# Hybrid decoder block on one core: another order for the last attention jobs and the first feed-forward units

## Chip, cores and metric

The kernel runs on one NeuronCore of a Trainium2 chip. The metric is the device time of one execution in microseconds (us), as the median of several runs; before the change it is 583.53 us (three runs, 583.22 to 583.65).

## What is computed

One layer, with x of 512 tokens by 1024 (float32), cut to what matters here:

```python
h = rms_norm(x, g_mix_norm)
z = h @ w_in                      # q, k, v of 8 heads, gate logits, gMLP channels
o_attn = g0 * o_cmp + g1 * o_sel + g2 * o_win       # compressed, selected, window attention
o_mix = gelu(zu) * spatial(rms_norm(gelu(zv)))
o = concat([rms_norm(o_attn, g_out[:512]), rms_norm(o_mix, g_out[512:])])
x = x + o @ w_out
h = rms_norm(x, g_ffn_norm)
x = x + square(relu(h @ w_ff1)) @ w_ff2              # w_ff1 1024 x 4096, w_ff2 4096 x 1024
```

## The kernel before

Tokens lie in four tiles of 128 (t = 0 to 3). The five engines run programs of their own, each in its written order, and wait on counting semaphores. Every float32 product is made of three matmuls (`three`, lines 427 to 429) over operands split into a high and a low part: ScalarE writes the high part, VectorE the rest. Weights come by DMA in units of 128 x 1024 into a ring of four `raw` slots; `unit_hi` (line 1039, ScalarE) and `unit_lo` (line 1563, VectorE) split them.

The **attention** goes in steps over heads and branches on TensorE. Between the steps stand jobs, named by kind, token tile and half:

- ("attno", t, h): twelve matmuls that project the attention rows of tile t on half h of the model width. VectorE's `add` (line 1555) puts the result on the residual `xs`, and counts `added`.
- ("attn", t, 0): four transposes (line 1779) of the attention rows of tile t into a PSUM bank. They wait for `o_evac`, which VectorE counts after the last additions (`combine`, line 1543) of the tile's sums.
- ("ffn", t, i): four transposes of half i of the rows of tile t for the feed-forward, which VectorE's `ffn_rows` (line 1222) makes from `xs` when both the addition of ("attno", t, i) and the norm weights are there.

A transposed bank is taken out by `ht_hi_evac` (line 785, ScalarE) and `ht_lo_evac` (line 1228, VectorE), which count `ht_half` and `ht_done`; of some ("ffn", t, 0), listed in `RAWS`, also by `raw_keep` (line 1044, ScalarE) as plain float32. `turn_back` (line 2085) are two transposes that bring finished attention sums into token order, after ScalarE's `ot_keep` (line 1073).

Behind the attention's loop stand the jobs of `TAIL`, in this order on TensorE: ("attno",2,1) and the last `turn_back`, ("attn",3,0), ("ffn",2,0), ("ffn",1,0), ("ffn",1,1), ("attno",3,0), ("attno",3,1), ("ffn",3,0), ("ffn",2,1); then feed-forward unit 0, ("ffn",3,1), unit 1, unit 2 and so on.

The **feed-forward** is a seven-product scheme over two token blocks (tiles 0 and 1, tiles 2 and 3) and two halves of the inner width. A unit is one `raw` slot of weights: 24 matmuls of 128 x 256 (`first_unit`) for the first matrix. Units 0 to 3 belong to product P2 (rows 0 to 255, second half of the width: ("ffn",0,1) and ("ffn",1,1)), units 4 to 7 to P1, units 8 and on use sums of rows (`form`, `form_high`, `form_low`) and weights that GpSimd's DMA adds up in the `raw` slot (line 680). A unit n waits for `w_lo` of its weights; the load of unit n+4 waits for the same split.

The order of VectorE behind the loop: `ffn_rows(2,0)`, `add(attno,2,1)`, `ht_lo_evac(attn,3,0)`, `ffn_rows(2,1)`, `ht_lo_evac(ffn,1,0)` and `(ffn,1,1)`, `add(attno,3,0)`, `ffn_rows(3,0)`, `ht_lo_evac(ffn,2,1)`, `late_difference(2)` (line 1604, a difference of two transposed halves), `add(attno,3,1)`, `ffn_rows(3,1)`, `unit_lo(2)`, `ht_lo_evac(ffn,3,1)`, `late_difference(3)`, `unit_lo(3)`. ScalarE: a wait for the last additions and the squares of attention tile 3 (line 770), `ht_hi_evac(attn,3,0)`, `raw_keep(2,0)`, for i = 0, 1 `raw_keep(1,i)` and `ht_hi_evac(ffn,1,i)`, squares of tile 2, `raw_keep(3,0)`, `ht_hi_evac(ffn,2,1)`, `unit_hi(2)`, `ht_hi_evac(ffn,3,1)`, `unit_hi(3)`, squares of tile 3. The weights of units 0 and 1 are split inside the attention's loop.

Of the kernel before, what the change touches and what calls it, by code (L numbers as in the profile page):

```python
# [14 lines left out]
NT = SEQ // P  # L15
# [36 lines left out]
NS = len(SPLITS)  # L52
# [27 lines left out]
N1 = BLOCK * sum(r[0] == 1 for r in ROUNDS)  # L80


def unit(n):

    stage, product, block, q, adding = ROUNDS[n // BLOCK]
    return stage, product, block * BLOCK + n % BLOCK, q, adding
# [17 lines left out]
def results_of(n):  # L104
# [13 lines left out]

RAWS = [(0, 0), (0, 1), (2, 0), (1, 0), (1, 1), (3, 0)]
FORMED = ["S1late2", "S1late3", "S3", "S2", "S4"]
FSPLIT = ["S1", "S2", "S4", "S3"]
FORM_STEPS = {5: "S3", 6: "S2", 7: "S4"}
# [9 lines left out]
KINDS = ["x", "mix", "attn", "ffn"]  # L134

HT = ([("x", u, k) for u in range(4) for k in range(2)] + [("mix", t, 0) for t in range(NT)]
      + [("attn", 0, 0), ("attn", 1, 0), ("ffn", 0, 0), ("ffn", 0, 1), ("attn", 2, 0), ("attn", 3, 0),
         ("ffn", 1, 0), ("ffn", 1, 1), ("ffn", 2, 1), ("ffn", 3, 1)])
HTN = {k: n for n, k in enumerate(HT)}


# [32 lines left out]
NV = len(STEPS)  # L174
# [37 lines left out]
def steps_of(k):  # L212
# [6 lines left out]
ENDS = {v + steps_of(k) - 1: k for k, v in JOBS.items()}  # L219
assert max(CHUNKS) < NV + LAG and len(CHUNKS) == sum(map(steps_of, JOBS))  # L220

TAIL = [("attno", 2, 1), ("attn", 3, 0), ("ffn", 2, 0), ("ffn", 1, 0), ("ffn", 1, 1), ("attno", 3, 0),
        ("attno", 3, 1), ("ffn", 3, 0), ("ffn", 2, 1), ("ffn", 3, 1)]
JOB_BANK = {k: JB[n % 2] for n, k in enumerate(JOBS)}
JOB_BANK.update({("ffn", 1, 0): 5, ("ffn", 1, 1): 6,
                 ("attno", 2, 1): 3, ("attn", 3, 0): 0, ("ffn", 2, 0): 4, ("ffn", 2, 1): 3, ("attno", 3, 0): 1,
                 ("attno", 3, 1): 2, ("ffn", 3, 0): 0, ("ffn", 3, 1): 1})
JOB = {k: n for n, k in enumerate(list(JOBS) + TAIL)}
JOB_KEY = list(JOB)
# [1 line left out]
ADD_NO = {k: n for n, k in enumerate(ADDS)}  # L231
# [4 lines left out]
def hybrid_block(nc, x, xt, w512, w_c, cmp_w1, cmp_w2, cmp_pe, sp_w, sp_b, g_cols, g_ffn, g_heads, g_sgu,  # L236
                 g_kc, rope, w_ff1, w_ff2, y):
    ctx = ExitStack()
    with ctx:
# [130 lines left out]
        w_hi, w_lo = sem("w_hi"), sem("w_lo")  # L370
# [37 lines left out]
        o_step, o_evac = sem("o_step"), sem("o_evac")  # L408
        job_done, added = sem("job_done"), sem("added")
        r2_step = sem("r2_step")  # L410
        raw_kept, formed = sem("raw_kept"), sem("formed")
# [49 lines left out]
        def job_taken(eng, k):  # L461
# [5 lines left out]
            else:  # L467
                eng.wait_ge(raw_kept, RAWS.index(k[1:]) + 1)

# [274 lines left out]
        def _(act):  # L744
# [34 lines left out]
            def ht_hi_evac(kind, t, i):  # L779
                if (kind, t, i) not in JOB:  # L780
                    act.wait_ge(filled, FILL["mixT", t, i] + 1)
                else:
                    act.wait_ge(job_done, JOB[kind, t, i] + 1)
                src, h, _ = halves_of(kind, t, i, ht_bank(kind, t, i))
                act.activation(h, src, ACT.Copy).then_inc(ht_half, 1)
# [255 lines left out]
            def raw_keep(t, i):  # L1041

                act.wait_ge(job_done, JOB["ffn", t, i] + 1)
                act.activation(ht_raw[:, 4 * i:4 * i + 4, t * P:t * P + P],
                               ps[:, JOB_BANK["ffn", t, i], :].rearrange("p (k s) -> p k s", k=4), ACT.Copy
                               ).then_inc(raw_kept, 1)
# [63 lines left out]
                    norm_sum("ffn", t, scr[:, :])  # L1110
            act.wait_ge(o_evac, 2 * NT)
            norm_sum("attn", 3, scr[:, 0:AW])
            ht_hi_evac("attn", 3, 0)
            raw_keep(2, 0)
            for i in range(2):
                raw_keep(1, i)
                ht_hi_evac("ffn", 1, i)
            act.wait_ge(added, ADD_NO["attno", 2, 1] + 1)
            norm_sum("ffn", 2, scr[:, :])

# [61 lines left out]
        def _(dve):  # L1182
# [34 lines left out]
            def ffn_rows(t, i):  # L1217

                cols = slice(i * AW, i * AW + AW)
                dve.wait_ge(grow_ffn_in, 16)  # L1220
                dve.wait_ge(added, ADD_NO["attno", t, i] + 1)
                dve.tensor_tensor(o_sb[:, t, cols], xs[:, t, cols], grow_ffn[:, cols], ALU.mult).then_inc(n_rows, 1)

            def ht_lo_evac(kind, t, i):
                n = HTN[kind, t, i]
                dve.wait_ge(ht_half, n + 1)
                src, h, l = halves_of(kind, t, i, ht_bank(kind, t, i))
                dve.tensor_tensor(l, src, h.bitcast(F32), ALU.subtract).then_inc(ht_done, 1)
# [317 lines left out]
            def add(kind, t, h):  # L1546

                c = slice(h * AW, h * AW + AW)
                dve.wait_ge(job_done, JOB[kind, t, h] + 1)
                if kind == "mixo":  # L1550
                    dve.wait_ge(x_again[t], 16)
                    dve.wait_ge(o_rstd, 1)
                else:
                    dve.wait_ge(o_rstd, t + 2)
                dve.scalar_tensor_tensor(out=xs[:, t, c], in0=ps[:, JOB_BANK[kind, t, h], :],
                                         scalar=stat(rstd, {"mixo": "mix", "attno": "attn"}[kind], t),
                                         in1=xs[:, t, c], op0=ALU.mult, op1=ALU.add).then_inc(added, 1)
# [8 lines left out]
            for w in range(NV + LEAD + LAG + BACK + 1):  # L1566
                s = w - LEAD
                k = ENDS.get(s)
# [22 lines left out]


            ffn_rows(2, 0)
            add("attno", 2, 1)
            ht_lo_evac("attn", 3, 0)
            ffn_rows(2, 1)
            ht_lo_evac("ffn", 1, 0)
            ht_lo_evac("ffn", 1, 1)

            def late_difference(t):  # L1600

                cut = (slice(None), slice(0, 4), slice(t * P, t * P + P))
                dve.wait_ge(raw_kept, RAWS.index((t, 0)) + 1)
                dve.tensor_tensor(ht_raw[:, 4:8, t * P:t * P + P], ht_raw[cut],
# [46 lines left out]
            def form(s):  # L1651

                dve.wait_ge(formed, FORMED.index(s))
                if s == "S3":
                    dve.wait_ge(raw_kept, len(RAWS))
                    dve.tensor_tensor(form_raw("S3"), form_raw("S2"), form_raw("S3"), ALU.subtract).then_inc(formed, 1)
# [102 lines left out]
        def _(pe):  # L1759
# [316 lines left out]
            def turn_back(i):  # L2076

                pe.wait_ge(ot_evac, i + 1)
                if i == 0:
                    wait_free(pe, LAST_FILL[3])  # L2080
                elif i % 2 == 0:
                    pe.wait_ge(o_evac, i // 2)
                for e in range(2):
                    c = i % 2 * 256 + e * P
                    mm = pe.transpose(ps[:, 7, c:c + P], ot_sb[:, i % 2, e, :], ident[:, :])
                mm.then_inc(back_done, 1)
# [15 lines left out]
            def job(k, c):  # L2102

                before = [p for p in JOB_KEY[:JOB[k]] if JOB_BANK[p] == JOB_BANK[k]]
                if c == 0 and before:
                    job_taken(pe, before[-1])
                if k in TRANSPOSED:
                    rows_t(k[0], k[1], (k[2],))
                else:
                    mm = project(*k, c)  # L2110
                    if c == 3:
                        mm.then_inc(job_done, 1)
# [18 lines left out]
                    turn_back((v - LAG - BACK) // 4)  # L2131

            pe.wait_ge(pt_lo, NV)
            for k in TAIL[:-1]:
                for c in range(4 if k in ADD_NO else 1):
                    job(k, c)
                if k == TAIL[0]:
                    turn_back(NV // 4 - 1)


            pe.wait_ge(o_evac, 2 * NT)

            def row_form(product):

                if product in ("P5", "P6", "P3"):
# [6 lines left out]
            def first_unit(n):  # L2152

                _, product, k, _, _ = unit(n)
                j = n % BLOCK
                h, l = row_form(product)
                for e in range(2):
                    for kt in range(4):
                        c = slice(512 * e + P * kt, 512 * e + P * kt + P)
                        mm = three(pe, psum_of(n)[:, e * TH:e * TH + TH], w_hi_sb[:, FS[j], c], w_lo_sb[:, FS[j], c],  # L2160
                                   h[:, kt, :], l[:, kt, :], kt == 0, kt == 3)
                mm.then_inc(w_used, 1)

            def wait_rows(product):

                if product == "P2":
                    pe.wait_ge(ht_done, HTN["ffn", 1, 1] + 1)
                elif product == "P4":
                    pe.wait_ge(ht_done, len(HT))
                elif product != "P1":  # L2170
                    pe.wait_ge(form_lo, FSPLIT.index({"P5": "S1", "P6": "S2", "P3": "S4", "P7": "S3"}[product]) + 1)
# [6 lines left out]
                else:  # L2178
                    pe.wait_ge(combined, COMBINED[BANK_FREE[product], k] + 1)

            for n in range(N1):
                r = n // BLOCK
                if r < 7 and n % BLOCK == 0:
                    wait_rows(unit(n)[1])
                if r >= 2:
                    bank_taken(n - 2 * BLOCK)
                elif n == 0:
                    pe.wait_ge(raw_kept, RAWS.index((2, 0)) + 1)
                elif n == BLOCK:
                    pe.wait_ge(raw_kept, len(RAWS))  # L2190
                    pe.wait_ge(formed, 2)
                    pe.wait_ge(added, len(ADDS))
                pe.wait_ge(w_lo, NS + n + 1)
                first_unit(n)
                if n == 0:
                    job(("ffn", NT - 1, 1), 0)

            def piece(n, e, i):

# [10 lines left out]
            for n in range(N1, NU - BLOCK):  # L2210
                _, product, k, _, _ = unit(n)
# [90 lines left out]
```

## Time and profile before

| what | value |
|---|---|
| median of three runs | 583.53 us |
| the profiled execution | 584.08 us, its span 582.3 us |
| TensorE busy | 567.3 us, 97% of the span |
| VectorE, ScalarE busy | 441.0 us (76%), 358.3 us (62%) |
| granted TensorE clock, mean | 0.999 |
| the stretch of the change | about 251 to 277 us |

The profile is of one execution. PE is TensorE's matmuls (transposes too), PEld its weight loads, DVE VectorE, ACT ScalarE, POOL GpSimd, SP SyncE. The ends of matmuls are modelled, and neighbours overlap in the rows, so the distance between two starts tells how long one keeps the engine. In the timeline neighbours of one kind are merged into a row with their count, and the idle time before a row stands in brackets with what ended it. Times in a timeline count from the start of the span.

### The profile page before, as it was taken

How to read it: one execution, taken by the hardware profiler on the slowest of the kernel's cores; microseconds unless marked ns; L12 is line 12 of the kernel's file. 1: busy time of each engine (PE TensorE's matmuls, PEld its weight loads, DVE VectorE, ACT ScalarE, POOL GpSimd, SP SyncE). 2: the span in 40 equal slices, each digit the busy share in tenths (PEclk: the TensorE clock that was granted, in tenths of full speed). 3: DMA queues.
4: the chain of work that ended last, by engine and by line, in shares of the span. 5: the costliest groups of instructions: out<-in, count | busy, mean ns of one | idle time of the engine just before them, and what ended most of it. 6: DMA issues, size and time to landing. Idle time of an engine off the chain costs nothing.

```text
span 582.3 us, 9217 instructions
## 1 busy us (share of the span) xinstructions
PE 567.3 (97%) x3433; PEld 495.7 (85%) x3433; DVE 441.0 (76%) x721; ACT 358.3 (62%) x644; POOL 129.2 (22%) x209
## 2 busy tenths in 40 slices
PE   8999999999998999999999999999999999999997
PEld 6877777788777887879999999999988888888886
DVE  3699890686877889857868675566699996999674
ACT  6766661737767777745763486733696655646651
POOL 0560000002544453501220102312023032020200
PEclk9999999999999999999999999999999999999999
DMA  8933346342212111003996958997699889877862
GB/s 305 348 101 105 113 145 221 140 167 88 73 38 74 36 38 38 0 2 84 204 191 186 206 181 162 186 200 167 192 146 191 207 174 205 233 140 227 194 199 109
DMA packets 25164, 87.56 MB, mean 150 GB/s; under 512 B 3024, under 2 KB 3312, under 8 KB 25120
## 3 DMA queue, kind: packets, MB, share of 16 engines
q0 software_dynamic: 9856, 35.38, 32.9%
q1 hardware_dynamic: 15120, 51.59, 25.8%
q8 instruction: 28, 0.46, 0.3%
q14 instruction: 16, 0.13, 0.1%
q10 hardware_dynamic: 144, 0.00, 0.0%
HBM read 84.87 MB, written 2.10 MB: 149 GB/s over the span
## 4 chain that ended last, share of the span: by engine, by line
PE 84%; DVE 5%; DMA 3%; POOL 2%; issue 2%; ACT 2%; SPq 1%; DVEq 0%; ACTq 0%
PE ps L427 24%; PE ps L429 23%; PE ps L428 23%; PE ps L2071 2%; PE ps L2052 2%; DMA xT<-in_xt 2%; PE ps L2013 1%; DMA pe_sb<-in_cmp_pe 1%; PE ps L1922 1%; PE ps L2014 1%; PE ps L1779 1%; POOL rope_k L606 1%; DVE w_lo_sb L1199 1%; PE ps L1885 1%; PE ps L1974 1%
## 5 line engine op out<-in xcount | busy, mean ns | idle before, releaser
L1039 ACT ACTIVATE w_hi_sb<-raw 128x1024 fp32r<-128x1024 f32 x112 | 118.7, 1060 | 114.9 <-PE ps L429 88.5
L1563 DVE TENSOR_TENSOR w_lo_sb<-raw,w_hi_sb 128x1024 fp32r<-128x1024 f32 x112 | 137.1, 1225 | 64.6 <-ACT w_hi_sb L1039 64.4
L680 POOL DMA_DIRECT2D raw<-in_w_ff x64 | 55.5, 868 | 237.5 <-DVE w_lo_sb L1563 213.4
L427 PE MATMUL ps<-w_hi_sb,a_hi 128*128 128x512 f32 x224 | 87.1, 389 | 0.0
L428 PE MATMUL ps<-w_lo_sb,a_hi 128*128 128x512 f32 x224 | 87.1, 389 | 0.0
L429 PE MATMUL ps<-w_hi_sb,a_lo 128*128 128x512 f32 x224 | 87.1, 389 | 0.0
L427 PE MATMUL ps<-w_hi_sb,ht_hi 128*128 128x512 f32 x192 | 78.2, 407 | 1.1 <-DVE w_lo_sb L1195 0.8
L427 PE MATMUL ps<-ht_hi,w_hi_sb 128*128 128x256 f32 (+1 forms) x272 | 79.1, 291 | 0.0
L429 PE MATMUL ps<-ht_hi,w_lo_sb 128*128 128x256 f32 (+1 forms) x272 | 78.8, 290 | 0.0
L428 PE MATMUL ps<-ht_lo,w_hi_sb 128*128 128x256 f32 (+1 forms) x272 | 78.7, 290 | 0.0
L429 PE MATMUL ps<-w_hi_sb,ht_lo 128*128 128x512 f32 x192 | 75.2, 391 | 0.0
L428 PE MATMUL ps<-w_lo_sb,ht_hi 128*128 128x512 f32 x192 | 75.1, 391 | 0.0
L427 PE MATMUL ps<-S_hi,w_hi_sb 128*128 128x256 f32 x192 | 54.3, 283 | 0.0
L428 PE MATMUL ps<-S_lo,w_hi_sb 128*128 128x256 f32 x192 | 54.3, 283 | 0.0
L429 PE MATMUL ps<-S_hi,w_lo_sb 128*128 128x256 f32 x192 | 54.3, 283 | 0.0
L429 PEld LDWEIGHTS ps<-ht_hi,w_lo_sb 128*128 128x128 f32 x272 | 52.1, 192 | 0.7
L427 PEld LDWEIGHTS ps<-ht_hi,w_hi_sb 128*128 128x128 f32 x272 | 52.1, 192 | 0.7
L428 PEld LDWEIGHTS ps<-ht_lo,w_hi_sb 128*128 128x128 f32 x272 | 52.2, 192 | 0.6
L427 PEld LDWEIGHTS ps<-w_hi_sb,a_hi 128*128 128x128 f32 x224 | 42.0, 188 | 8.8
L428 PEld LDWEIGHTS ps<-w_lo_sb,a_hi 128*128 128x128 f32 x224 | 42.0, 188 | 8.7
L429 PEld LDWEIGHTS ps<-w_hi_sb,a_lo 128*128 128x128 f32 x224 | 42.0, 188 | 8.7
L427 PEld LDWEIGHTS ps<-w_hi_sb,ht_hi 128*128 128x128 f32 x192 | 36.1, 188 | 9.2 <-issue 3.2
(238 smaller groups left out, 1139.4 us busy)
## 6 DMA issues: line engine op xcount, KB each, us to landing
raw<-in_w_ff POOLq DMA_DIRECT2D x64, 512.0 KB, 6.5
raw<-in_w_ff SPq DMA_DIRECT2D x48, 512.0 KB, 4.3
raw<-in_w SPq DMA_DIRECT2D x23, 512.0 KB, 4.5
xs<-in_x SPq DMA_DIRECT2D x8, 512.0 KB, 7.8
raw<-in_cmp_w SPq DMA_DIRECT2D x8, 512.0 KB, 4.6
xT<-in_xt SPq DMA_DIRECT2D x3, 512.0 KB, 9.2
raw<-in_w_c SPq DMA_DIRECT2D x4, 304.0 KB, 2.8
out_y<-xs SPq DMA_DIRECT2D x2, 512.0 KB, 3.1
```

The source lines that it names most:

```text
L427: pe.matmul(out, l_hi, r_hi, start=start, stop=False)
L428: pe.matmul(out, l_hi, r_lo, start=False, stop=False)
L429: return pe.matmul(out, l_lo, r_hi, start=False, stop=stop)
L606: pool.tensor_tensor(out, bc(table, shape), bc(g, shape), ALU.mult).then_inc(rope_made, 1)
L680: pool.dma_start(raw[:, n % RAW, :], (w_ff1, w_ff2)[stage - 1][k, q], accum_op=ALU.add, max_dma_last_dim=8192).then_inc(raw_added[n % RAW] ...
L1039: act.activation(w_hi_sb[:, FS[j], :], raw[:, j, :], ACT.Copy).then_inc(w_hi, 1)
L1199: last = dve.scalar_tensor_tensor(out=l[:, k, :], in0=r[:, k, :], scalar=gcol(n, k), in1=h[:, k, :].bitcast(F32), op0=ALU.mult, op1=ALU.su ...
L1563: dve.tensor_tensor(w_lo_sb[:, FS[j], :], raw[:, j, :], w_hi_sb[:, FS[j], :].bitcast(F32), ALU.subtract).then_inc(w_lo, 1)
L1779: last = pe.transpose(ps[:, bank, k * P:k * P + P], src[:, k * P:k * P + P], ident[:, :])
L1885: last = pe.transpose(ps[:, fill_bank(j), k * P:k * P + P], src, ident[:, :])
L2052: mm = pe.transpose(ps[:, 4 + v % 2, k * P:k * P + P], p_sb[:, v % PB, k * P:k * P + P], ident[:, :])
L2071: mm = pe.matmul(out, v_sb[:, k, c, g, :, :].rearrange("p e d -> p (e d)"), pt_sb[c][:, part, slot, :, :].rearrange("p e s -> p (e s)"), s ...
```

## The change

TensorE: the transposes ("ffn",1,0) come first, then the first two of four parts of ("attno",2,1), the last `turn_back`, ("ffn",1,1), the other two parts, ("attn",3,0), ("ffn",2,0); then unit 0, both last projections ("attno",3,0) and (3,1), unit 1, and the transposes ("ffn",3,0), ("ffn",2,1), ("ffn",3,1) in one run, then unit 2. ("ffn",2,0) goes to PSUM bank 7 instead of 4, since unit 0 now writes bank 4. On ScalarE `raw_keep(1,i)` and `ht_hi_evac(ffn,1,i)` come ahead of `ht_hi_evac(attn,3,0)` and `raw_keep(2,0)`; on VectorE the two `ht_lo_evac(ffn,1,i)` come ahead of `add(attno,2,1)`. The rest of both orders stays. The lists `RAWS` and `HT`, from which counts are worked out, follow.

```diff
-RAWS = [(0, 0), (0, 1), (2, 0), (1, 0), (1, 1), (3, 0)]
+RAWS = [(0, 0), (0, 1), (1, 0), (1, 1), (2, 0), (3, 0)]
...
-      + [("attn", 0, 0), ("attn", 1, 0), ("ffn", 0, 0), ("ffn", 0, 1), ("attn", 2, 0), ("attn", 3, 0),
-         ("ffn", 1, 0), ("ffn", 1, 1), ("ffn", 2, 1), ("ffn", 3, 1)])
+      + [("attn", 0, 0), ("attn", 1, 0), ("ffn", 0, 0), ("ffn", 0, 1), ("attn", 2, 0),
+         ("ffn", 1, 0), ("ffn", 1, 1), ("attn", 3, 0), ("ffn", 2, 1), ("ffn", 3, 1)])
...
-TAIL = [("attno", 2, 1), ("attn", 3, 0), ("ffn", 2, 0), ("ffn", 1, 0), ("ffn", 1, 1), ("attno", 3, 0),
+TAIL = [("ffn", 1, 0), ("ffn", 1, 1), ("attno", 2, 1), ("attn", 3, 0), ("ffn", 2, 0), ("attno", 3, 0),
         ("attno", 3, 1), ("ffn", 3, 0), ("ffn", 2, 1), ("ffn", 3, 1)]
...
-                 ("attno", 2, 1): 3, ("attn", 3, 0): 0, ("ffn", 2, 0): 4, ("ffn", 2, 1): 3, ("attno", 3, 0): 1,
+                 ("attno", 2, 1): 3, ("attn", 3, 0): 0, ("ffn", 2, 0): 7, ("ffn", 2, 1): 3, ("attno", 3, 0): 1,
...
             norm_sum("attn", 3, scr[:, 0:AW])
-            ht_hi_evac("attn", 3, 0)
-            raw_keep(2, 0)
             for i in range(2):
                 raw_keep(1, i)
                 ht_hi_evac("ffn", 1, i)
+            ht_hi_evac("attn", 3, 0)
+            raw_keep(2, 0)
...
             ffn_rows(2, 0)
+            ht_lo_evac("ffn", 1, 0)
+            ht_lo_evac("ffn", 1, 1)
             add("attno", 2, 1)
             ht_lo_evac("attn", 3, 0)
             ffn_rows(2, 1)
-            ht_lo_evac("ffn", 1, 0)
-            ht_lo_evac("ffn", 1, 1)
...
             pe.wait_ge(pt_lo, NV)
-            for k in TAIL[:-1]:
-                for c in range(4 if k in ADD_NO else 1):
-                    job(k, c)
-                if k == TAIL[0]:
-                    turn_back(NV // 4 - 1)
-            pe.wait_ge(o_evac, 2 * NT)
...
-            for n in range(N1):
+            job(TAIL[0], 0)
+            for c in range(4):
+                job(TAIL[2], c)
+                if c == 1:
+                    turn_back(NV // 4 - 1)
+                    job(TAIL[1], 0)
+            for k in TAIL[3:]:
+                if k == ("attno", 3, 0):
+                    wait_rows(unit(0)[1])
+                    pe.wait_ge(w_lo, NS + 1)
+                    first_unit(0)
+                if k == ("ffn", NT - 1, 0):
+                    pe.wait_ge(w_lo, NS + 2)
+                    first_unit(1)
+                for c in range(4 if k in ADD_NO else 1):
+                    job(k, c)
+            pe.wait_ge(raw_kept, RAWS.index((2, 0)) + 1)
+
+            for n in range(2, N1):
...
-                elif n == 0:
-                    pe.wait_ge(raw_kept, RAWS.index((2, 0)) + 1)
                 elif n == BLOCK:
...
                 first_unit(n)
-                if n == 0:
-                    job(("ffn", NT - 1, 1), 0)
```

## Rows read from the trace of the kernel before

**Rows 1.** The page, first part: busy us, share of span, instructions of TensorE

```profile
PE 567.3 (97%) x3433; PEld 495.7 (85%) x3433; DVE 441.0 (76%) x721; ACT 358.3 (62%) x644; POOL 129.2 (22%) x209
```

**Rows 2.** Waits of PE, 240 us to the end: total, times, longest us

```profile
PE ps L1779 <- DVE o_sb L1543: 1.0, 1, 1.0
PE ps L1779 <- DVE o_sb L1222: 0.7, 1, 0.7
```

**Rows 3.** Timeline of PE, 250 to 258: start, us, engine, line, operation, shapes

```profile
251.12 0.47 PE L427 MATMUL ps<-w_hi_sb,ht_hi 128*128 128x512 f32 x1
...
253.97 0.38 PE L2085 MATMUL ps<-ident,ot_sb 128*128 128x128 f32 x2
255.39 2.13 PE L1779 MATMUL ps<-ident,o_sb 128*128 128x128 f32 x16 [1.04 <-DVE o_sb L1543]
257.55 0.47 PE L427 MATMUL ps<-w_hi_sb,ht_hi 128*128 128x512 f32 x1
```

**Rows 4.** Timeline of PE, 263 to 269

```profile
263.12 1.04 PE L1779 MATMUL ps<-ident,o_sb 128*128 128x128 f32 x8
263.91 0.36 PE L427 MATMUL ps<-ht_hi,w_hi_sb 128*128 128x256 f32 x1
...
266.75 0.28 PE L429 MATMUL ps<-ht_hi,w_lo_sb 128*128 128x256 f32 x1
267.77 0.63 PE L1779 MATMUL ps<-ident,o_sb 128*128 128x128 f32 x4 [0.74 <-DVE o_sb L1222]
268.15 0.36 PE L427 MATMUL ps<-ht_hi,w_hi_sb 128*128 128x256 f32 x1
```

**Rows 5.** Stretches: length, busy us of each engine, granted PE clock, DMA share, GB/s

```profile
254.00:256.00 2.00, 0.96 (x8) 0.54 (x6) 1.51 (x4) 0.63 (x2) 0.00 (x0) 1.00 0.00 0
...
275.00:280.00 5.00, 5.00 (x44) 5.00 (x44) 4.54 (x5) 2.32 (x3) 1.64 (x3) 1.00 0.97 168
```

**Rows 6.** Timeline of DVE, 254 to 257

```profile
254.46 0.88 DVE L1543 TENSOR_TENSOR o_sb<-o_sb,ps 128x256 f32<-128x256 f32 x2 [3.44 <-PE ps L2085]
255.25 0.69 DVE L1222 TENSOR_TENSOR o_sb<-xs,grow_ffn 128x512 f32<-128x512 f32 x1
...
256.71 0.69 DVE L1228 TENSOR_TENSOR ht_lo<-ps,ht_hi 128x512 fp32r<-128x512 f32 x1
```

**Rows 7.** Timeline of ACT, 255 to 259

```profile
255.37 0.63 ACT L770 ACTIVATE scr<-o_sb 128x512 bf16<-128x512 f32 x1 [3.77 <-DVE o_sb L1543]
...
256.08 0.60 ACT L785 ACTIVATE ht_hi<-ps 128x512 fp32r<-128x512 f32 x1
...
257.66 0.61 ACT L785 ACTIVATE ht_hi<-ps 128x512 fp32r<-128x512 f32 x1
...
258.62 0.63 ACT L785 ACTIVATE ht_hi<-ps 128x512 fp32r<-128x512 f32 x1
```

**Rows 8.** Timeline of ACT and DVE, 263 to 268

```profile
263.76 0.60 ACT L1044 ACTIVATE ht_raw<-ps 128x512 f32<-128x512 f32 x1 [3.49 <-PE ps L1779]
...
264.88 0.69 DVE L1228 TENSOR_TENSOR ht_lo<-ps,ht_hi 128x512 fp32r<-128x512 f32 x1 [2.74 <-ACT ht_hi L785]
...
266.08 0.74 DVE L1555 SCALAR_TENSOR_TENSOR xs<-ps,rstd,xs 128x512 f32<-128x512 f32 x1
266.93 0.69 DVE L1222 TENSOR_TENSOR o_sb<-xs,grow_ffn 128x512 f32<-128x512 f32 x1
267.54 1.22 DVE L1563 TENSOR_TENSOR w_lo_sb<-raw,w_hi_sb 128x1024 fp32r<-128x1024 f32 x1
```

**Rows 9.** Timeline of DVE, 269 to 272: the low weights of unit 3

```profile
270.26 1.22 DVE L1563 TENSOR_TENSOR w_lo_sb<-raw,w_hi_sb 128x1024 fp32r<-128x1024 f32 x1
```

**Rows 10.** Timelines of POOL and ACT: load and high part of unit 8

```profile
273.52 0.98 POOL L680 DMA_DIRECT2D raw<-in_w_ff  x1 [16.51 <-DVE w_lo_sb L1563]
...
280.01 1.06 ACT L1039 ACTIVATE w_hi_sb<-raw 128x1024 fp32r<-128x1024 f32 x1 [1.82 <-PE ps L429]
```

**Rows 11.** Line 2036, the transposes that warm TensorE: duration ns min/median/max, first and last start

```profile
L2036 PE MATMUL ps<-ident x36: 272/273/475, 1.6 to 143.2; 128*128 128x128 f32 x36
```

## What I predict, before the changed kernel has run

> **What bounds the kernel now.** I read the page's first part, then the waits of TensorE, then the timeline of the stretch that the change touches. TensorE is busy 97% of the span [rows 1], so the time moves only by idle time of TensorE that is taken away or added. From 240 us to the end it waits just twice, both times at the transposes of line 1779 for VectorE, 1.0 and 0.7 us by the modelled ends of the matmuls before [rows 2]. I take the issue times instead. In the timeline the first is the gap between the two transposes that turn the last attention sums back (253.97, 0.22 us for the two) and the transposes of the third token tile's attention rows, ("attn",3,0), at 255.39 [rows 3]: 255.39 - 253.97 - 0.22 = 1.20 us idle. The second lies between the last matmul of feed-forward unit 0 (266.75, issued 0.12 us apart, so free at 266.87) and the transposes ("ffn",3,1) at 267.77 [rows 4]: 0.90 us idle. After that TensorE issues without a gap: the stretch from 275 to 280 is 5.00 of 5.00 us busy [rows 5], and the list has no wait beyond. So an earlier or later start of units 2, 3, 4 moves the end one for one, as long as weights and sums stay ahead. At most 1.20 + 0.90 = 2.1 us can be won here.
>
> **Lengths that I use.** Two jobs of four transposes take 263.91 - 263.12 = 0.79 us, one 268.15 - 267.77 = 0.38 [rows 4]: 0.40 each. The twelve matmuls of ("attno",2,1) take 253.97 - 251.12 = 2.85 us, the 24 of ("attno",3,0) and (3,1) 263.12 - 257.55 = 5.57 [rows 3, 4]. A unit of 24 matmuls takes 266.87 - 263.91 = 2.96 us, 2.88 behind another unit.
>
> **First part: block 1's transposes ahead, sums turned back inside ("attno",2,1).** From 251.12 TensorE now does ("ffn",1,0) (0.40) and half of the job (1.43): the turning back starts at 252.95. Before, ("attn",3,0) started 1.42 us after it (the two additions of line 1543 begin 0.49 after it and take 0.88) [rows 3, 6], so it may start at 254.37. TensorE meanwhile does the two transposes (0.22), ("ffn",1,1) (0.40) and the other half (1.43), to 255.00. The first stall, 1.20 us, goes, with 0.63 us to spare. VectorE's ("ffn",2,0) rows follow the additions as before and are ready before 255.40. ("attn",3,0) and ("ffn",2,0) end at 255.80. The 16 transposes that stood in one run for 2.16 us (255.39 to 257.55) now cost 1.6, since the wait and the change of work inside that run do not recur: another 0.5 us.
>
> **Second part: unit 0 right behind them.** Unit 0 (product P2) waits for `ht_done` of ("ffn",1,1). What makes those rows? ScalarE first sits in its wait for the last additions and squares attention tile 3 (start 1.40 us after the turning back, 0.71 to the next instruction), then `raw_keep(1,0)`, `ht_hi_evac` (1,0), `raw_keep(1,1)`, `ht_hi_evac` (1,1): steps of 0.48 us (257.66 to 258.62 is two), the last 0.63 long [rows 7]. Then VectorE's `ht_lo_evac`, 0.69 [rows 6], and 0.05 at each hand-over. Sum: 1.40 + 0.71 + 3 x 0.48 + 0.63 + 0.05 + 0.69 + 0.05 = 4.97 us behind the turning back, 257.92. TensorE is there at 255.80: a **new stall of 2.1 us**. The early transposes buy nothing, because their evacuations queue on ScalarE behind the wait for the additions. On VectorE the two `ht_lo_evac` also come ahead of `add(attno,2,1)` and `ht_lo_evac(attn,3,0)`; the latter then ends near 259.2, hidden by unit 0, which runs to 260.88. The 24 matmuls of the last two projections end at 266.45, unit 1 at 269.41 (its weights and unit 0's were split during the attention).
>
> **Third part: the last jobs.** Here lies most of the cost. VectorE's own order is not changed: after `ffn_rows(3,0)` come `ht_lo_evac(ffn,2,1)`, `late_difference(2)`, and only then `add(attno,3,1)` and `ffn_rows(3,1)`, which makes the rows of the last transposes ("ffn",3,1). The first of these waits for the transposes ("ffn",2,1), and these now stand behind unit 1. So while unit 1 runs VectorE is idle, though the sums of ("attno",3,1) are ready. Before, from the first transpose of ("ffn",3,0) at 263.12 the chain was: ScalarE keeps (3,0) at 263.76 and evacuates (2,1), VectorE at 264.88, its difference, the addition at 266.08, the rows at 266.93, ("ffn",3,1) at 267.77 [rows 4, 8]. Each starts when the one before ends, none waits for anything else, so its 4.65 us hold wherever it starts. Unit 0 hid 2.96 of them and 0.79 were transposes, 0.90 showed. In the changed kernel nothing stands between ("ffn",2,1) and ("ffn",3,1): 4.65 - 0.79 = **3.86 us idle**, and ("ffn",3,1) starts at 269.41 + 4.65 = 274.06. Behind it unit 2 needs its low weights, which VectorE makes after the rows: 267.54 to 268.76 before [rows 8], 5.64 us behind the first transpose, with 0.05 at 275.10. TensorE would be ready at 274.06 + 0.38 = 274.44: **0.66 us more**. Before, unit 1 covered this. Unit 3's low weights ended at 271.48, 3.71 us behind the start of ("ffn",3,1) [rows 4, 9], so at 277.77, before unit 2 ends at 278.06: hidden by only 0.3 us. Unit 4 starts at 275.10 + 0.08 + 5.76 = 280.94, before it was 268.15 + 0.08 + 3 x 2.88 = 276.87. The difference is **+4.07 us**; as a ledger, -1.20 - 0.90 - 0.5 + 2.1 + 3.86 + 0.66 = +4.0.
>
> **What hangs on the queues behind.** VectorE splits unit 4's weights some 2.5 us later against TensorE than before, and GpSimd issues the accumulating load of unit 8 behind that (273.52 before, 0.3 after the split), so at about 279.9. Before, it was landed when ScalarE read it at 280.01, within 6.5 us [rows 10]; now that is 286.4 or a little later, where unit 4 sets the slot free at 283.9. With 1.06 and 1.23 us for the split, unit 8 is ready by 289, and TensorE reaches it at 292.5. SyncE's loads of units 6 and 7 follow the splits of units 2 and 3 and have over 5 us too. I put this at nothing; the DMA engines are full there (share 0.97 from 275 to 280 [rows 5]), and if that load took 4 us longer, 292.7, it would cost 0.2 and each one behind it more.
>
> **The clock.** The granted clock reads 1.00 from 254 to 256, around the 1.20 us of idle time, and from 275 on [rows 5]. No row shows a gap of 3.9 us. The first transposes of the program, on an engine that had done nothing, lasted up to 475 ns against the median of 273 [rows 11], so a slower pace behind idle time exists. Of the two levels, 2.4 GHz is the 1.00 of the rows and 1.2 GHz doubles an issue interval. If the clock fell in the 3.9 us gap, half of unit 2 up to all of it would run at that pace: 1.4 to 2.9 us more.
> The Trainium skill, "TensorE: Matmul & The Clock Gate", Part 1, says that "the default state is throttled, and activity releases the throttle"; by it a long enough gap costs twice, once as idle time and once as slow matmuls. No run here shows it yet; that is the second rival below.
>
> **Rivals.** (1) The forecast: two stalls of 2.1 us in sum are replaced by three of 6.6, of which 0.5 is won back, +4.1 us. Against the profiled execution's 584.08 us (span 582.3) that is 588.2; it stands 0.55 over the median of 583.53, which gives 587.6. Bounds: the chain to unit 0 may be 0.5 shorter, and each of three restarts may cost 0.2 more: 587.0 to 588.3. (2) The same, and the clock falls in the long gap: 589.0 to 590.5. For it speaks the length of the gap, against it that 0.8 us of transposes stand before it and 0.4 after it, and that the 1.20 us gap did nothing. (3) Not slower: both chains are hidden. Unit 1's 2.96 us would cover the addition and rows of (3,1), 0.75 + 0.69 us, and the two old stalls go for 2.1: 581.4. It decides on whether VectorE gets to `add(attno,3,1)` while unit 1 runs; the order of its program says that it can't. (4) The change half works: the last chain is hidden, unit 0's wait is not. -1.20 - 0.90 - 0.5 + 2.1 = -0.5: 583.0, no difference. (5) The three stalls, and late loads on top: 588.0 to 589.
>
> **How the numbers follow.** (1) 0.71, (2) 0.13, (3) 0.06, (4) 0.04, (5) 0.06. A measurement of this kernel can tell about 0.2%, 1.2 us, from no change. Faster: 0.06. Same: 0.04. Slower: 0.90. The range takes in all of (1) and (5) and the lower part of (2); below it reaches 0.4 further, which is how far the three runs of before lie apart (583.22 to 583.65): 586.6 to 589.6.
>
> **What would show it.** Right: in the timeline of the changed kernel 16 transposes are no longer one run, the wait before ("attn",3,0) is gone; TensorE waits about 2 us for VectorE's line of `ht_lo_evac` before unit 0; between the two last groups of transposes lies a gap of 3.9 us that ends on the rows of line 1222, with VectorE idle for about 3 us during unit 1; then 0.7 us on unit 2's low weights; no other wait of TensorE to the end. Wrong: VectorE works on line 1555 during unit 1, or unit 0 starts within 0.5 us of the transposes, or TensorE waits again beyond unit 4, or a stretch with a granted clock under 1.00.

## The result, and the profile after

The changed kernel takes 588.98 us (median of four executions, 588.34 to 590.19) against 583.40 (median of four, 583.22 to 583.65): a ratio of 1.0098, with a 95% interval of 1.0085 to 1.011. It is 5.6 us slower. The profiled execution took 588.66 us, its span is 586.9 us, and its mean granted clock 0.997 against 0.999 before.

The waits of TensorE from 240 us on (total, times, longest us), against [rows 2]:

```profile
PE ps L1779 <- DVE o_sb L1222: 3.6, 1, 3.6
PE ps L427 <- DVE ht_lo L1228: 1.8, 1, 1.8
PE ps L427 <- DVE w_lo_sb L1563: 0.5, 1, 0.5
```

The wait for the additions (line 1543) is gone, the one for the rows of line 1222 has grown from 0.7 to 3.6, and two are new: one for the low part of transposed rows, one for low weights. The timeline of TensorE shows where, first from the last turning back to unit 0, against [rows 3]:

```profile
252.25 0.38 PE L2085 MATMUL ps<-ident,ot_sb 128*128 128x128 f32 x2
252.47 0.60 PE L1779 MATMUL ps<-ident,o_sb 128*128 128x128 f32 x4
...
254.30 1.03 PE L1779 MATMUL ps<-ident,o_sb 128*128 128x128 f32 x8
257.10 0.38 PE L427 MATMUL ps<-ht_hi,w_hi_sb 128*128 128x256 f32 x1 [1.76 <-DVE ht_lo L1228]
```

("attn",3,0) follows at 254.30 without a wait. The eight transposes keep the engine 0.79 us, so until unit 0 at 257.10 it idles 2.01 us. Then the last transposes and unit 2, against [rows 4]:

```profile
268.40 1.03 PE L1779 MATMUL ps<-ident,o_sb 128*128 128x128 f32 x8
273.05 0.63 PE L1779 MATMUL ps<-ident,o_sb 128*128 128x128 f32 x4 [3.61 <-DVE o_sb L1222]
274.18 0.54 PE L427 MATMUL ps<-ht_hi,w_hi_sb 128*128 128x256 f32 x1 [0.51 <-DVE w_lo_sb L1563]
274.52 0.42 PE L428 MATMUL ps<-ht_lo,w_hi_sb 128*128 128x256 f32 x1
...
277.30 0.41 PE L429 MATMUL ps<-ht_hi,w_lo_sb 128*128 128x256 f32 x1
277.51 0.34 PE L427 MATMUL ps<-ht_hi,w_hi_sb 128*128 128x256 f32 x1
...
278.64 0.28 PE L427 MATMUL ps<-ht_hi,w_hi_sb 128*128 128x256 f32 x1
```

From 268.40 to 273.05 are 4.65 us, the same chain as before, now bare: 3.86 us idle. Another 0.75 us pass until unit 2 (273.05 + 0.38 to 274.18). And unit 2 is slow: behind its first matmul (0.54 us) the next fourteen last 0.41 to 0.42 us and start 0.21 apart instead of 0.12. Unit 3 starts at 278.64, 4.46 us behind unit 2, where 2.96 were due. The stretches of one us (length, PE busy, PEld, DVE, ACT, POOL, then the granted clock, DMA share, GB/s):

```profile
273.00:274.00 1.00, 0.63 (x4) 0.42 (x4) 1.00 (x1) 0.29 (x1) 0.00 (x0) 1.00 0.00 0
274.00:275.00 1.00, 0.82 (x4) 0.85 (x5) 0.69 (x3) 1.00 (x2) 0.00 (x0) 0.60 0.00 0
275.00:276.00 1.00, 1.00 (x6) 1.00 (x6) 1.00 (x3) 1.00 (x2) 0.00 (x0) 0.50 0.81 172
276.00:277.00 1.00, 1.00 (x7) 1.00 (x6) 0.97 (x3) 1.00 (x3) 0.00 (x0) 0.50 0.86 352
277.00:278.00 1.00, 1.00 (x8) 1.00 (x7) 0.95 (x3) 1.00 (x2) 0.00 (x0) 0.69 0.28 49
278.00:279.00 1.00, 1.00 (x10) 1.00 (x9) 1.00 (x2) 0.28 (x2) 0.20 (x1) 1.00 0.79 291
```

The granted clock falls to 0.50, the level of 1.2 GHz, soon after TensorE works again, and is back at 278. VectorE beside it, against [rows 6, 8]:

```profile
263.87 0.69 DVE L1222 TENSOR_TENSOR o_sb<-xs,grow_ffn 128x512 f32<-128x512 f32 x1
270.16 0.69 DVE L1228 TENSOR_TENSOR ht_lo<-ps,ht_hi 128x512 fp32r<-128x512 f32 x1 [5.60 <-ACT ht_hi L785]
270.77 0.68 DVE L1604 TENSOR_TENSOR ht_raw<-ht_raw,ps 128x512 f32<-128x512 f32 x1
271.36 0.74 DVE L1555 SCALAR_TENSOR_TENSOR xs<-ps,rstd,xs 128x512 f32<-128x512 f32 x1
272.21 0.69 DVE L1222 TENSOR_TENSOR o_sb<-xs,grow_ffn 128x512 f32<-128x512 f32 x1
272.82 1.22 DVE L1563 TENSOR_TENSOR w_lo_sb<-raw,w_hi_sb 128x1024 fp32r<-128x1024 f32 x1
```

It idles 5.60 us before the low part of ("ffn",2,1), all through unit 1, while the sums of ("attno",3,1) lie ready for line 1555, two places further on in its order.

**A measure for single profiles.** Every profiled execution reaches the last but one turning back at its own time (249.16 before, 248.57 after), for reasons upstream of the change. So I compare the stretch from there to the first matmul of unit 8, a landmark that all the kernels have: 249.16 to 288.39 is 39.23 us before, 248.57 to 293.04 is 44.47 after, 5.24 more. Behind it, from unit 8 to the end, all profiled executions of all kernels here need 293.85 to 293.94 us. Whatever the change did is in the stretch, and nothing is given back or lost later.

### The profile page after: what moved, and what is told of

Read it like the earlier page. It is cut to its first block, busy times and chain, and to the rows that moved or that the text cites. A ratio compares the mean times of both kernels' runs of the same rounds, so it can differ in the third digit from the quotient of the medians.

```text
span 586.9 us, 9218 instructions
## 1 busy us (share of the span) xinstructions
PE 568.1 (97%) x3433; PEld 497.1 (85%) x3433; DVE 441.3 (75%) x721; ACT 358.1 (61%) x644; POOL 129.7 (22%) x209
## 4 chain that ended last, share of the span: by engine, by line
PE 83%; DVE 6%; DMA 3%; ACT 2%; POOL 2%; issue 2%; SPq 1%; DVEq 0%; ACTq 0%
PE ps L427 23%; PE ps L429 23%; PE ps L428 23%; PE ps L2071 2%; PE ps L2052 2%; DMA xT<-in_xt 2%; PE ps L2013 1%; PE ps L1922 1%; DMA pe_sb<-in_cmp_pe 1%; PE ps L2014 1%; POOL rope_k L606 1%; DVE w_lo_sb L1199 1%; PE ps L1779 1%; PE ps L1885 1%; PE ps L1974 1%
```

## The experiments

Times are medians, with the kernel before run beside them (583.23 to 583.50). Diffs are against the changed kernel unless another is named. `warm(n, b)` in them issues n transposes of the identity into PSUM bank b; a "fall" is a stretch behind a gap in which the granted clock reads 0.50.

### Filling the long gap

```diff
                 for c in range(4 if k in ADD_NO else 1):
                     job(k, c)
+                if k == ("ffn", 2, 1):
+                    warm(30, 6)
```

> The changed kernel with 30 transposes of the identity into the free PSUM bank 6 (their result is not used) between the transposes (ffn,2,1) and (ffn,3,1), where TensorE idles 3.86 us. 30 x 0.11 = 3.3 us of work that nothing waits for. Theory (the clock fell because of the long gap): the granted clock stays 1.00 behind it, unit 2 takes 2.9 instead of 4.5 us, the waits stay where they are, so 588.98 - 1.5 = 587.5 us. Rival (unit 2 was slow for another reason, such as the split of weights and the loads beside it): unit 2 again takes 4.5 us and the time stays at 589.0.

588.42 us (587.06 to 589.26), ratio 1.0085 (1.0071 to 1.0099); the stretch is 44.47 us as without the filler. Unit 2 ran at full pace: behind its first matmul they last 0.28 us again.

```profile
275.39 0.36 PE L427 MATMUL ps<-ht_hi,w_hi_sb 128*128 128x256 f32 x1 [0.51 <-DVE w_lo_sb L1563]
275.59 0.28 PE L428 MATMUL ps<-ht_lo,w_hi_sb 128*128 128x256 f32 x1
```

But in this execution the clock fell elsewhere, behind the 2.0 us gap before unit 0 (stretches; length, PE busy, granted clock, DMA share, GB/s):

```profile
256.00:258.00 2.00, 1.20 (x10) 1.00 0.00 0
258.00:259.00 1.00, 1.00 (x9) 0.66 0.00 0
259.00:260.00 1.00, 1.00 (x6) 0.50 0.00 0
260.00:261.00 1.00, 1.00 (x7) 0.50 0.00 0
261.00:262.00 1.00, 1.00 (x5) 0.64 0.05 16
```

So the filler keeps unit 2 at its pace, as the theory had it, and the splits and loads beside unit 2, which the rival named, did not slow it. But the expected 587.5 was reached by one execution only (587.06): two of the others have a mean clock of 0.997 and 0.996, and the third took 588.40 us at 1.0, for which there is no trace. The median doesn't settle what a fall costs; the next run does.

### Filling both gaps

```diff
+                    warm(17, 4)
                     wait_rows(unit(0)[1])
                     pe.wait_ge(w_lo, NS + 1)
                     first_unit(0)
...
+                if k == ("ffn", 2, 1):
+                    warm(32, 6)
```

> The changed kernel with 17 transposes of the identity before unit 0 and 32 between (ffn,2,1) and (ffn,3,1); their results are not used, and all waits stay. The run with only the second filler had unit 2 at full pace, but in the profiled execution the clock fell behind the 2.0 us gap before unit 0 instead (0.66, 0.50, 0.50, 0.64 from 258 to 262). Theory (a fall needs a gap of about 2 us or more, and costs 1.6 to 1.9 us): every execution at a granted clock of 1.00, 587.1 us, within 0.5 of each other. Rival (the falls have nothing to do with the gaps): some executions again at 0.997 and 588.5.

587.15 us (586.74 to 587.9), ratio 1.0069 (1.0055 to 1.0082), the mean clock 1.0, 1.0, 0.999, 1.0 and 1.0 in the five executions. The only wait of TensorE left to the end is the one for unit 2's weights, 0.5 us. The stretch is 42.98 us against 44.47: the fall cost 1.49 us. The first filler's, 44.47 too, holds one fall behind the other gap, so it cost the same there. The theory holds for the clock and the median. The executions lie 1.2 us apart, not the 0.5 that I had written, at a full clock; only the profiled one has a trace, so where that width arises is not shown.

### VectorE's order alone

```diff
             ffn_rows(3, 0)
-            ht_lo_evac("ffn", 2, 1)
-            late_difference(2)
             add("attno", 3, 1)
             ffn_rows(3, 1)
+            ht_lo_evac("ffn", 2, 1)
+            late_difference(2)
             unit_lo(2)
```

> The changed kernel with VectorE's addition of (attno,3,1) and its rows (ffn,3,1) ahead of the low part of (ffn,2,1) and the late difference of tile 2; nothing else. Theory (each gap is the chain through ScalarE and VectorE that comes last): the 3.9 us gap before (ffn,3,1) goes, the three groups of transposes run in one, but unit 2's low weights now come last: high part behind the keep of (3,0) and the high part of (2,1) on ScalarE, then low part behind two others on VectorE, 4.2 us behind the first transpose, which leaves 3.1 us idle in place of 3.9 + 0.5. So 1.5 us less, 587.5, if the clock still falls, 586.0 if a gap of 3.1 us does not let it fall. Rival (the order of VectorE alone made the loss): all 4.5 us and the 1.5 us of clock go, 583.0.

585.84 us (585.78 to 589.65), ratio 1.0049 (1.0036 to 1.0063). The twelve transposes are one run now, and behind them comes the wait that the theory named:

```profile
270.80 1.47 PE L1779 MATMUL ps<-ident,o_sb 128*128 128x128 f32 x12
275.11 0.36 PE L427 MATMUL ps<-ht_hi,w_hi_sb 128*128 128x256 f32 x1 [2.85 <-DVE w_lo_sb L1563]
```

By issue times this gap is 275.11 - 270.80 - 1.18 = 3.13 us (eight transposes keep the engine 0.79 us, so twelve 1.18), where 3.1 was expected. By the mean clock of each execution the five divide: three at 1.0 took 585.78 to 585.84 us, one at 0.997 took 587.47, the profiled one at 0.993 took 589.65, and its trace shows two falls, behind both gaps. So the theory's figures are met, 586.0 without a fall and 587.5 with one; the median is one without, and that of the changed kernel one with. The rival, that this order alone made the loss (583.0), fell: moving the additions removes one link, and the next latest, the weights of unit 2, takes its place.

### The tail mended

```diff
 ScalarE:
+            unit_hi(2)
+            unit_hi(3)
             raw_keep(3, 0)
             ht_hi_evac("ffn", 2, 1)
-            unit_hi(2)
             ht_hi_evac("ffn", 3, 1)
-            unit_hi(3)
 VectorE:
             ffn_rows(3, 0)
-            ht_lo_evac("ffn", 2, 1)
-            late_difference(2)
+            unit_lo(2)
             add("attno", 3, 1)
             ffn_rows(3, 1)
-            unit_lo(2)
+            unit_lo(3)
+            ht_lo_evac("ffn", 2, 1)
+            late_difference(2)
             ht_lo_evac("ffn", 3, 1)
             late_difference(3)
-            unit_lo(3)
```

> The changed kernel with the addition and rows of (3,1) ahead on VectorE, and with the splits of units 2 and 3 ahead of the keep of (3,0) on ScalarE and between the additions on VectorE, so that they run beside (attno,3,1) and unit 1. Theory: both waits at the end of the jobs and the slow clock behind them go: 3.86 + 0.66 + 1.5 = 6.0 us less, 583.0; the wait of 2.0 us before unit 0 stays. Rival (the weights or the sums are late next): a new wait of 1 us or more at units 2 to 4, 584 or more.

582.61 us (582.2 to 583.94), ratio 0.9989 (0.998 to 0.9997); the stretch is 38.44 us, 6.03 less than with the changed kernel, where 6.0 were expected. The wait of 1.8 us for line 1228, before unit 0, is the only one left. The 2.0 us gap is still there, and two of eleven executions took 583.9 us at a mean clock of 0.997, the others 582.2 to 583.6 at 0.999 or 1.0.

### The tail and unit 0 mended

On top of the diff above:

```diff
 ScalarE:
-            act.wait_ge(o_evac, 2 * NT)
-            norm_sum("attn", 3, scr[:, 0:AW])
             for i in range(2):
                 raw_keep(1, i)
                 ht_hi_evac("ffn", 1, i)
+            act.wait_ge(o_evac, 2 * NT)
+            norm_sum("attn", 3, scr[:, 0:AW])
 VectorE, in the last round but one of its loop:
+                if s == NV + LAG + 1:
+                    ht_lo_evac("ffn", 1, 0)
...
             ffn_rows(2, 0)
-            ht_lo_evac("ffn", 1, 0)
             ht_lo_evac("ffn", 1, 1)
```

> As the run with the tail mended, and ScalarE keeps and splits (ffn,1,0) and (ffn,1,1) before it waits for the last additions, VectorE takes the low part of (ffn,1,0) ahead of the additions. Theory: the 2.0 us before unit 0 go too, 581.0, and TensorE waits nowhere from 250 us on; that is 2.4 below the kernel before. Rival (ScalarE's wait was not what held the rows, or the squares of attention tile 3 that now come later hold the projections' additions): 583 again, with the wait on another line.

580.65 us (580.31 to 580.84), ratio 0.9953 (0.994 to 0.9965). The list of waits of TensorE from 240 us on is empty, and the stretches say the same (length, busy us of PE, PEld, DVE, ACT, POOL, clock, DMA share, GB/s):

```profile
250.00:270.00 20.00, 20.00 (x139) 18.43 (x139) 12.07 (x19) 10.53 (x19) 0.75 (x2) 1.00 0.19 54
270.00:290.00 20.00, 20.00 (x169) 20.00 (x169) 18.12 (x21) 14.27 (x20) 6.53 (x8) 1.00 0.85 158
```

The stretch is 36.41 us, 2.03 less than with the tail alone, 2.82 less than before. This is the fastest kernel of the study. TensorE's order is that of the change; what the change lacked is the order of the other two engines. The two moves, ScalarE's wait and VectorE's first low part, were not run apart.

### Unit 1 between the last transposes

```diff
-                if k == ("ffn", NT - 1, 0):
+                if k == ("ffn", NT - 1, 1):
                     pe.wait_ge(w_lo, NS + 2)
                     first_unit(1)
```

> The changed kernel with unit 1 between (ffn,2,1) and (ffn,3,1) instead of ahead of (ffn,3,0). Theory: unit 1 covers 2.96 us of the 3.86 us chain, and what is left is 0.9 us; unit 2's low weights are late by 0.7 us still; the clock falls at most behind the gap before unit 0. So 588.98 - 2.96 - 1.6 = 584.4, or 0.6 less if the restart hides part of the weights. Rival (another wait takes the place): 586 or more.

584.97 us (583.85 to 585.7), ratio 1.0026 (1.0016 to 1.0035). Its waits:

```profile
PE ps L427 <- DVE ht_lo L1228: 1.8, 1, 1.8
PE ps L1779 <- DVE o_sb L1222: 0.7, 1, 0.7
PE ps L427 <- DVE w_lo_sb L1563: 0.5, 1, 0.5
```

The long one is 0.7 again, as in [rows 2]: one unit covers all but 0.9 us of the chain, wherever it stands. The stretch is 40.12 us, 4.35 less than the changed kernel's 44.47: 2.96 for the cover, and the other 1.39 is near the 1.49 of the fall that this trace doesn't have. The median is 0.6 above the expectation. The ten executions divide into five of 583.9 to 584.5 us and five of 585.4 to 585.7; the profiled one is of the second kind (585.69), shows no fall of the clock, and came to the stretch at 249.94, 1.4 us later than the changed kernel's. Of the other four, two (585.56 and 585.58) have a mean clock of 0.997, as one fall gives; for the two at 1.0 (585.42 and 585.70) there is no trace.

### VectorE's order in the kernel before

Against the kernel before:

```diff
             ffn_rows(3, 0)
-            ht_lo_evac("ffn", 2, 1)
-            late_difference(2)
             add("attno", 3, 1)
             ffn_rows(3, 1)
+            ht_lo_evac("ffn", 2, 1)
+            late_difference(2)
             unit_lo(2)
```

> The kernel before with one thing changed: on VectorE the addition and the rows of (3,1) ahead of the low part of (ffn,2,1) and the late difference. Theory: in both kernels the last chain is VectorE's order; here the 0.9 us stall before (ffn,3,1) goes and nothing takes its place, since unit 1 still covers unit 2's weights: 583.4 - 0.9 = 582.5. Rival (the rows are late for the addition itself): 583.4, unchanged.

582.31 us (581.96 to 583.62), ratio 0.9984 (0.9976 to 0.9993), the stretch 38.30 us, 0.93 less. Two moved lines are worth what the second stall of before was, 0.90. The same move in the changed kernel left a wait of 2.85 us, since no unit stood behind the transposes to cover unit 2's weights (3.13 us by issue times).

### The first part alone, and with the old evacuations

Both have the early transposes and the turning back inside the job, but unit 0 and unit 1 where they were before:

```diff
-                if k == ("attno", 3, 0):
-                    wait_rows(unit(0)[1])
-                    pe.wait_ge(w_lo, NS + 1)
-                    first_unit(0)
-                if k == ("ffn", NT - 1, 0):
-                    pe.wait_ge(w_lo, NS + 2)
-                    first_unit(1)
+                if k == ("ffn", NT - 1, 1):
+                    pe.wait_ge(raw_kept, RAWS.index((2, 0)) + 1)
+                    wait_rows(unit(0)[1])
+                    pe.wait_ge(w_lo, NS + 1)
+                    first_unit(0)
```

> The first part of the change alone: block 1's transposes ahead, the sums turned back inside (attno,2,1), and the evacuations in the changed order, but unit 0 between (ffn,2,1) and (ffn,3,1) and unit 1 behind, as before. Theory: the 1.20 us stall and 0.5 us of the old run of transposes go, the 0.9 us before (ffn,3,1) stays: 583.4 - 1.7 = 581.7. Rival (part of the loss comes from the first part): 583 or more.

585.93 us (584.8 to 586.61), ratio 1.0041 (1.0029 to 1.0054). The theory fell and its rival came: 1.7 us were to be won, 2.7 were lost. The next job, ("attno",3,0), waits for the low part of ("attn",3,0):

```profile
258.52 0.76 PE L427 MATMUL ps<-w_hi_sb,ht_hi 128*128 128x512 f32 x1 [3.11 <-DVE ht_lo L1228]
```

VectorE makes it at 257.70, behind the two low parts of block 1 and `add(attno,2,1)`; in the changed kernel unit 0 hides this. By issue times the gap is 258.52 - 254.38 - 0.79 = 3.35 us. The clock fell behind it too: of the five executions the three at 0.996 or 0.997 took 585.93 to 586.61 us, the two at 1.0 took 584.80 and 584.88. So without the fall the loss is 1.6 us. The second kernel puts the evacuations back into their old order (attention tile 3 and ("ffn",2,0) first, on both engines, with `RAWS` and `HT` as before).

> The first part of the change alone, with the evacuations on ScalarE and VectorE in the order of the kernel before (attention tile 3 and (ffn,2,0) first, block 1 behind). With the changed order (attno,3,0) waited 3.1 us for the low part of (attn,3,0), which came behind four evacuations of block 1. Theory: the chain from the last turning back over the additions, the transposes (attn,3,0) and their two evacuations to (attno,3,0) is the bound; its last link is now covered by (ffn,2,0) alone, since block 1's transposes have gone ahead, so about 1.3 us of waiting are left before (attno,3,0) and 0.9 before (ffn,3,1): 582.7 us. Rival (the turning back inside the job is what costs): 585 as with the changed order.

582.83 us (582.63 to 584.1), ratio 0.9989 (0.9981 to 0.9998), stretch 38.64. The wait is there; by issue times it is 256.21 - 254.10 - 0.79 = 1.32 us, where 1.3 was expected:

```profile
256.21 0.47 PE L427 MATMUL ps<-w_hi_sb,ht_hi 128*128 128x512 f32 x1 [1.07 <-DVE ht_lo L1228]
```

From the last turning back at 252.06 to this job are 4.15 us; before they were 257.55 - 253.97 = 3.58 [rows 3], with all work of TensorE between. So taking block 1's transposes ahead uncovers the evacuation of ("attn",3,0), and of the 1.7 us only 0.6 are won. The rival (585) fell: the turning back inside the job isn't what costs.

### Two moves in the kernel before

Against the kernel before, VectorE's order as above and

```diff
                 for c in range(4 if k in ADD_NO else 1):
                     job(k, c)
-                if k == TAIL[0]:
-                    turn_back(NV // 4 - 1)
+                    if k == TAIL[0] and c == 1:
+                        turn_back(NV // 4 - 1)
```

> The kernel before with two moves only: the last turning back between the second and third part of (attno,2,1), and VectorE's addition and rows of (3,1) ahead of the low part of (ffn,2,1) and the late difference. Block 1's transposes and both first units stay where they were. Theory: the half job behind the turning back covers the additions (1.43 + 0.22 us against 1.42), the three groups of transposes behind (attn,3,0) still cover its evacuations, and unit 0 the sums: both stalls go, 2.1 us, 581.1. Rival (the gain of the best run so far, 580.65, needs the early transposes and units): 582.3, as with VectorE's move alone.

581.18 us (580.95 to 582.44), ratio 0.9963 (0.9949 to 0.9976), stretch 37.04, 2.19 less than before:

```profile
253.21 0.38 PE L2085 MATMUL ps<-ident,ot_sb 128*128 128x128 f32 x2
254.82 1.95 PE L1779 MATMUL ps<-ident,o_sb 128*128 128x128 f32 x16
256.92 0.47 PE L427 MATMUL ps<-w_hi_sb,ht_hi 128*128 128x512 f32 x1 [0.15 <-DVE ht_lo L1228]
```

Both stalls of before are gone with two small moves; the fastest kernel wins 0.6 us more in the stretch. So most of the gain needs neither the early transposes nor the early units.

| kernel | time, us | stretch, us | stretch against before |
|---|---|---|---|
| before | 583.4 | 39.23 | |
| changed | 588.98 | 44.47 | +5.24 |
| long gap filled | 588.42 | 44.47 | +5.24 |
| both gaps filled | 587.15 | 42.98 | +3.75 |
| changed, VectorE's order | 585.84 | 44.51 | +5.28 |
| first part, new evacuations | 585.93 | 42.27 | +3.04 |
| unit 1 between | 584.97 | 40.12 | +0.89 |
| first part, old evacuations | 582.83 | 38.64 | -0.59 |
| tail mended | 582.61 | 38.44 | -0.79 |
| before, VectorE's order | 582.31 | 38.30 | -0.93 |
| before, two moves | 581.18 | 37.04 | -2.19 |
| tail and unit 0 mended | 580.65 | 36.41 | -2.82 |

A time is a median, a stretch that of the one profiled execution. The stretches of the changed kernel, of the long gap filled and of the first part with new evacuations hold one fall of the clock each, that of the changed kernel with VectorE's order two, the others none.

## Why the prediction was right, and where it was not

**Direction, place and causes: right.** I forecast slower by 4.1 us, through three stalls; it is 5.6, through the same three and a slower clock. The runs removed the stalls by what the reasoning named: the last two together, with the fall behind them (the tail mended, 6.03 us), then the one before unit 0 (2.03 us).

**The first stall, 1.20 us, gone: right.** ("attn",3,0) follows 2.05 us behind the turning back, as worked out (255.00 - 252.95), with no wait.

**The stall before unit 0, 2.1 us: right, measured 2.01.** Unit 0 starts 4.85 us behind the turning back instead of 4.97. ScalarE shows the queue; the rows against [rows 7]:

```profile
253.65 0.63 ACT L770 ACTIVATE scr<-o_sb 128x512 bf16<-128x512 f32 x1 [2.63 <-DVE o_sb L1543]
...
254.28 0.57 ACT L1044 ACTIVATE ht_raw<-ps 128x512 f32<-128x512 f32 x1
254.76 0.58 ACT L785 ACTIVATE ht_hi<-ps 128x512 fp32r<-128x512 f32 x1
```

It idles 2.63 us with the first of block 1's transposes ready since about 251, then takes them in steps of 0.48. The run with unit 0 mended took away 2.03 us by moving that wait behind them and VectorE's first low part ahead.

**The chain before ("ffn",3,1), 3.86 us: right**, 4.65 from start to start in both traces.

**Unit 2's weights, 0.66 us: right, measured 0.75.** The queues behind: right, no wait beyond unit 4; unit 8's load was issued at 278.80 instead of my 279.9 and was there when its slot came free.

**The sum without the clock**: +4.07 forecast, +3.75 measured with both gaps filled. The 0.3 that is missing is 0.11 up to the last turning back (3.68 us behind the last but one; before it was 4.81, and by my working 1.02 less, 3.79), 0.12 from there to unit 0, and 0.19 since the row of unit 0, projections and unit 1 needed 11.30 us (257.10 to 268.40), not 2.96 + 5.57 + 2.96 = 11.49; the 0.09 more before unit 2 goes the other way.

**The clock: the likeliest case left it out, and that was the step that failed.** The forecast of 587.6 was case (1); what came was case (2), with 0.13 of the chance, and a price of 1.49 us, at the lower end of my 1.4 to 2.9. 588.98 lies 0.02 under the 589.0 to 590.5 that I gave to it; it is inside my whole range, 586.6 to 589.6, because I had stretched that for late loads, which did not come, and for the lower part of case (2). So the range held partly by luck. And of my signs of being wrong one was there: a stretch with a granted clock under 1.00. I argued that 1.20 us of idle time had done nothing and that transposes stand before and behind the gap. The runs showed that the clock falls behind the gap of 3.86 us in the profiled execution, and no longer when the gap is filled; the mean clocks of the other three, 0.997, 0.997 and 0.994, say that they had falls too, though not behind which gap; and behind the 2.0 us gap it falls in some executions and not in others.
The Trainium skill's rule ("TensorE: Matmul & The Clock Gate", Part 1) that the default state is throttled and activity releases it agrees with this: the slow stretch lies behind the gap, on work, and ends by itself while TensorE is busy.

**A step that I did not see** because unit 0 covered it: the low part of ("attn",3,0) comes late by the new order of the evacuations. My text had it "hidden by unit 0", which is right, but it counted the early transposes as a gain of 0.5 us and did not say that without unit 0 the new order of their evacuations costs a gap of 3.35 us, and even the old order one of 1.32. The first part alone shows it.

## What to carry to other kernels

When work of one engine is moved ahead to cover a stall, write down the order of the other engines beside it: the kernel loses where another engine, in its own order, waits for something that now comes later, with the work that is due queued behind that wait. Here the moved work was right and the orders of ScalarE and VectorE were not; with them mended the same move went from +5.6 to -2.8 us. And price a gap of TensorE twice, once as idle time and once, with a chance that in these runs rose with its length, as slow work behind it: here 1.5 us, in all four executions with gaps of 2.0 and 3.9 us, in about a quarter of those with nothing longer than 2.0. Last, try the small moves on the kernel before first: two of them won 2.2 of the 2.8 us.

## What the runs showed of the hardware

- A fall of the granted clock behind a gap: 0.50 for about two microseconds with part of one on each side, 1.49 us lost (44.47 - 42.98 of the stretch). In the traces it came behind gaps of 2.0, 3.1, 3.3 and 3.9 us, not behind the gaps of 1.2 us before and 1.3 us in the first part with old evacuations. The 2.0 us gap was followed by one in the profiled executions of the first filler and of VectorE's order, and by none in those of the changed kernel, of the mended tail and of unit 1 between. By the mean clock (0.997 or less) there was a fall in 6 of 25 executions whose longest gap is the 2.0 us one (first filler, tail mended, unit 1 between), in 2 of 5 with 3.1 us beside it, in 3 of 5 with 3.3 us, and in 4 of 4 with 3.9 us beside it.
- It begins not in the gap but at its end or later, on busy slices: in the first part alone at the first matmul behind the gap (258.5), with the first filler about 1.5 us behind it (the gap ends at 256.80, the slices of 0.2 us read 1.00 up to 258.2), and in the changed kernel 1.1 us behind the long gap, with the first matmul of unit 2 (274.2).
- The mean clock of an execution tells of it, roughly: 0.997 for one fall and 0.993 for two in the profiled executions of the changed kernel and of VectorE's order. The first transposes of the program lasted up to 475 ns [rows 11], and TensorE got through 5 to 7 of them in each of the first three microseconds and 11 in the fourth, all at a reading of 1.00 (kernel before, 1.61 to 5.60), so the reading does not cover all.
- The time to the last but one turning back varies by 1.7 us between profiled executions (248.26 to 249.94), the rest behind unit 8 by 0.1. Differences under 1 us are seen in stretches between common landmarks, not in spans.
